# A decoder layer on one core: the down projection and final norm on token tiles of 344, 440 and 248 columns in place of three of 344

## What is computed

```
up = rmsnorm(x, g_ffn) @ w_up
upc, ffn_buf_new = causal_conv(ffn_buf, up, ffn_conv_w)
u, gt = jnp.split(upc, 2, axis=-1)
x = x + (jax.nn.silu(gt) * u) @ w_down
...
y_prompt = rmsnorm(xp, g_final)
y_sample = rmsnorm(xs, g_final)
```

## Time and profile before

| | us |
|---|---|
| median of 3 runs | 1088.61 (1086.8 to 1088.77) |
| the profiled execution, device time | 1090.33 |
| its span, first to last instruction | 1088.6 |
| TensorE busy in the span | 1063.2 (98%) |
| VectorE, ScalarE, GpSimd busy | 787.2, 511.7, 43.3 |

### The profile page before, as it was taken

One profiled execution on the slowest core, in us unless ns is written; L12 is line 12 of the kernel. 1 busy time (PEld: TensorE's weight loads), 2 busy tenths in 40 slices (PEclk: granted clock), 3 DMA queues, 4 the chain that ended last, 5 costly groups with the idle time before them and its releaser, 6 DMA issues.

```text
span 1088.6 us, 17576 instructions
## 1 busy us (share of the span) xinstructions
PE 1063.2 (98%) x6746; PEld 1031.6 (95%) x6746; DVE 787.2 (72%) x1310; ACT 511.7 (47%) x880; POOL 43.3 (4%) x165
## 2 busy tenths in 40 slices
PE   7999999999999999999999999999999999999995
PEld 6999988888999999999999999999999999999994
DVE  6954788898899888778768768777776554454457
ACT  7444344666444464454444444445444433333354
POOL 0100000000000000000000000000000000000004
PEclk9999999999999999999999999999999999999998
DMA  7311201114444112212211211311236856566504
GB/s 258 96 39 45 97 21 40 40 59 166 129 142 131 58 59 98 79 59 84 92 59 65 111 59 59 117 59 59 102 120 222 305 158 220 177 181 195 161 1 156
DMA packets 47395, 119.09 MB, mean 109 GB/s; under 512 B 5040, under 2 KB 25392, under 8 KB 47280
## 3 DMA queue, kind: packets, MB, share of 16 engines
q1 hardware_dynamic: 43904, 113.59, 31.2%
q10 hardware_dynamic: 3408, 4.38, 1.1%
HBM read 98.33 MB, written 20.66 MB: 109 GB/s over the span
## 4 chain that ended last, share of the span: by engine, by line
PE 65%; DVE 4%; issue 2%; ACT 1%; DMA 1%; SPq 1%; DVEq 0%; ACTq 0%
PE psum L2074 40%; PE psum L2098 18%; PE psum L2032 3%; PE psum L2050 2%; PE psum L1829 1%; DMA raw<-in_w 1%; DVE zb L1783 0%; PE psum L2131 0%; DVE zb L1144 0%; SPq L559 0%; SPq L625 0%; DVE x_sb L1487 0%; DVE att L1480 0%; ACT psum L1099 0%; DVE h_lo L1452 0%
## 5 line engine op out<-in xcount | busy, mean ns | idle before, releaser
L2074 PE MATMUL psum<-h_hi,w_lo 128*128 128x344 f32 x336 | 107.4, 320 | 0.0
L2074 PE MATMUL psum<-h_hi,act_lo 128*128 128x344 f32 x336 | 107.3, 319 | 0.0
L2074 PE MATMUL psum<-h_hi,act_hi 128*128 128x344 f32 x336 | 107.3, 319 | 0.0
L2074 PE MATMUL psum<-h_hi,w_hi 128*128 128x344 f32 x336 | 107.3, 319 | 0.0
L2074 PE MATMUL psum<-h_lo,act_hi 128*128 128x344 f32 x336 | 107.2, 319 | 0.0
L2074 PE MATMUL psum<-h_lo,w_hi 128*128 128x344 f32 x336 | 107.1, 319 | 0.0
L1150 DVE TENSOR_TENSOR w_lo<-raw,w_hi 128x1024 fp32r<-128x1024 f32 x50 | 61.1, 1224 | 56.1 <-ACT w_hi L726 55.8
L726 ACT ACTIVATE w_hi<-raw 128x1024 fp32r<-128x1024 f32 x51 | 53.7, 1056 | 80.0 <-PE psum L2098 58.4
L2098 PE MATMUL psum<-h_hi,w_hi 128*128 128x344 f32 x240 | 76.9, 321 | 1.2 <-DVE w_lo L1150 1.2
L2098 PE MATMUL psum<-h_hi,act_hi 128*128 128x344 f32 x240 | 77.1, 321 | 0.0
L2098 PE MATMUL psum<-h_lo,w_hi 128*128 128x344 f32 x240 | 76.7, 320 | 0.0
(11 more groups left out here) (313 smaller groups left out, 3039.0 us busy)
## 6 DMA issues: line engine op xcount, KB each, us to landing
raw<-in_w SPq DMA_DIRECT2D x111, 512.0 KB, 3.7
att<-in_w SPq DMA_DIRECT2D x26, 512.0 KB, 4.5
act_d<-att SPq DMA_DIRECT2D x20, 516.0 KB, 2.7
zb<-act_d SPq DMA_DIRECT2D x30, 344.0 KB, 4.1
x_sb<-in_x SPq DMA_DIRECT2D x8, 516.0 KB, 4.8
x_d<-x_sb ACTq DMA_DIRECT2D x12, 344.0 KB, 2.5
x_sb<-x_d SPq DMA_DIRECT2D x3, 1376.0 KB, 10.8
out_y<-x_sb SPq DMA_DIRECT2D x12, 344.0 KB, 2.5
```

Of the source, the lines that this page charges most:

```text
L2074: ins = mm(bank[to], a, b, start=(fresh and k == p == 0), stop=(k == HALF - 1 and p == 2), skip_group_check=True)
```

## The change

The down loop, the final blocks and the final norm take token tiles with edges at 0, 344, 784 and 1032: widths of 344, 440 and 248. All other parts keep tiles of 344. The number and order of instructions on each engine stay; the widths of operands and the sizes of transfers change. The running sums of squares, which lay in four places of 344 columns, lie in four of 440 (`DOWN_WIDTH`). The assertion of line 87 stays as it is and speaks of TW alone.

```
+DOWN_EDGES = (0, TW, 784, T)
+DOWN_WIDTH = max(b - a for a, b in zip(DOWN_EDGES, DOWN_EDGES[1:]))
...
-        stage = [s_flat[:, o:o + 2 * TW].rearrange("p (c t) -> p c t", c=2) for o in (0, 2 * TW)]
+        stage = [s_flat[:, o:o + 2 * DOWN_WIDTH].rearrange("p (c t) -> p c t", c=2) for o in (0, T)]
...
+        def down_tile(t):
+            return slice(DOWN_EDGES[t], DOWN_EDGES[t + 1])
+
+        def down_cols(t):
+            return slice(0, DOWN_EDGES[t + 1] - DOWN_EDGES[t])
...
-            return sq[:, g % 4, :]
+            return att[:, g % 4 * DOWN_WIDTH:g % 4 * DOWN_WIDTH + DOWN_EDGES[FIN_GROUPS[g][0] + 1] - DOWN_EDGES[FIN_GROUPS[g][0]]]
...
-                        sp.dma_start(x_sb[:, :, tile(t)], x2_d[:, :, tile(t)]).then_inc(x2_back[t], 16)
+                        sp.dma_start(x_sb[:, :, down_tile(t)], x2_d[:, :, down_tile(t)]).then_inc(x2_back[t], 16)
...
-                    ins = nc.gpsimd.tensor_tensor(x_sb[:, m, tile(t)], x_sb[:, m, tile(t)], rstd[:, tile(t)], ALU.mult)
+                    ins = nc.gpsimd.tensor_tensor(x_sb[:, m, down_tile(t)], x_sb[:, m, down_tile(t)], rstd[:, down_tile(t)], ALU.mult)
...
-                        xh, xl = h_hi[:, e + kk, tile(0)], h_lo[:, e + kk, tile(0)]
+                        xh, xl = h_hi[:, e + kk, down_cols(t)], h_lo[:, e + kk, down_cols(t)]
...
-                            ins = mm(down_ps[m], a, b, start=(g == kk == p == 0), stop=(g == DOWN_PAIRS - 1 and kk == 1 and p == 2))
+                            ins = mm(down_ps[m][:, down_cols(t)], a, b, start=(g == kk == p == 0), stop=(g == DOWN_PAIRS - 1 and kk == 1 and p == 2))
```

More of the change, by code:

```diff
@@ L458, in build @@
         job_ps = [psum[:, 512 * b:512 * b + TW] for b in range(3)]
-        fin_ps = [psum[:, 512 * b:512 * b + TW] for b in FIN_BANK]
+        fin_ps = [psum[:, 512 * b:512 * (b + 1)] for b in FIN_BANK]
+        square_ps = [psum[:, 512 * b:512 * (b + 1)] for b in range(3)]
         bank = {c: psum[:, 512 * b:512 * b + TW] for c, b in BANK.items()}
-        down_ps = [psum[:, 512 * b:512 * b + TW] for b in DOWN_BANK]
+        down_ps = [psum[:, 512 * b:512 * (b + 1)] for b in DOWN_BANK]
         gate_ps = [psum[:, 512 * b:512 * b + TW] for b in range(3, 6)]
@@ L558, in load_act @@
                     sp.wait_ge(act_split, i - 1)
-                sp.dma_start(stage[i % 2], act_d[2 * g:2 * g + 2, :, t * TW:(t + 1) * TW].rearrange("c p t -> p c t")).then_inc(act_landed[i % 2], 16)
+                sp.dma_start(stage[i % 2][:, :, down_cols(t)], act_d[2 * g:2 * g + 2, :, down_tile(t)].rearrange("c p t -> p c t")).then_inc(act_landed[i % 2], 16)
             for p in range(4):
@@ L635, in _ @@
                     sp.wait_ge(y_last_ready, n + 1 - by_pool)
-                sp.dma_start(outs["y"][:, m, tile(t)], x_sb[:, m, tile(t)]).then_inc(stored, 16)
+                sp.dma_start(outs["y"][:, m, down_tile(t)], x_sb[:, m, down_tile(t)]).then_inc(stored, 16)
             for t in range(NT):
@@ L1023, in split_act @@
                     act.wait_ge(half_done, 2 * (i - len(ENTRIES)) + 2)
-                nc.scalar.activation(h_hi[:, e:e + 2, tile(0)], stage[i % 2], ACT.Copy).then_inc(act_hi_ready, 1)
+                cols = down_cols(i // DOWN_PAIRS)
+                nc.scalar.activation(h_hi[:, e:e + 2, cols], stage[i % 2][:, :, cols], ACT.Copy).then_inc(act_hi_ready, 1)
             def split_last(c):
@@ L1093, in fin_square @@
                         act.wait_ge(fin_added, n - 2)
-                    dst = job_ps[n % 3]
+                    dst = square_ps[n % 3][:, down_cols(t)]
                 else:
@@ L1098, in fin_square @@
                     dst = fin_total(g)
-                nc.scalar.activation(dst, x_sb[:, m, tile(t)], ACT.Square).then_inc(fin_sq_ready, 1)
+                nc.scalar.activation(dst, x_sb[:, m, down_tile(t)], ACT.Square).then_inc(fin_sq_ready, 1)
             def fin_gain(t, m):
                 act.wait_ge(fin_sq_ready, KD * t + m + 1)
-                nc.scalar.activation(x_sb[:, m, tile(t)], x_sb[:, m, tile(t)], ACT.Copy,
+                nc.scalar.activation(x_sb[:, m, down_tile(t)], x_sb[:, m, down_tile(t)], ACT.Copy,
                                      scale=gain_fin[:, m:m + 1]).then_inc(fin_gain_done, 1)
@@ L1109, in fin_root @@
                 act.wait_ge(fin_sum_done, sum(u <= t for u, _ in FIN_GROUPS))
-                nc.scalar.activation(rstd[:, tile(t)], task_ps[:, 0:TW], ACT.Sqrt, bias=eps[:, 0:1],
+                nc.scalar.activation(rstd[:, down_tile(t)], task_ps[:, down_cols(t)], ACT.Sqrt, bias=eps[:, 0:1],
                                      scale=1.0 / D).then_inc(fin_root_done, 1)
@@ L1687, in act_rest @@
                 dve.wait_ge(act_hi_ready, i + 1)
-                V.tensor_tensor(h_lo[:, e:e + 2, tile(0)], stage[i % 2], f32(h_hi[:, e:e + 2, tile(0)]), ALU.subtract).then_inc(act_split, 1)
+                cols = down_cols(i // DOWN_PAIRS)
+                V.tensor_tensor(h_lo[:, e:e + 2, cols], stage[i % 2][:, :, cols], f32(h_hi[:, e:e + 2, cols]), ALU.subtract).then_inc(act_split, 1)
             def last_rest(c):
@@ L1700, in down_evac @@
                 src = down_ps[m] if n < NT * KD else fin_ps[n % 4]
-                V.tensor_tensor(x_sb[:, m, tile(t)], src, x_sb[:, m, tile(t)], ALU.add).then_inc(down_read, 1)
+                V.tensor_tensor(x_sb[:, m, down_tile(t)], src[:, down_cols(t)], x_sb[:, m, down_tile(t)], ALU.add).then_inc(down_read, 1)
             for name in FIRST_PARTS[0:3]:
@@ L1782, in fin_reciprocal @@
                 dve.wait_ge(fin_root_done, t + 1)
-                V.reciprocal(rstd[:, tile(t)], rstd[:, tile(t)]).then_inc(fin_rstd_ready, 1)
+                V.reciprocal(rstd[:, down_tile(t)], rstd[:, down_tile(t)]).then_inc(fin_rstd_ready, 1)
             def fin_add(t, m):
@@ L1793, in fin_add @@
                 total = fin_total(fin_group(t, m))
-                V.tensor_tensor(total, job_ps[n % 3], total, ALU.add).then_inc(fin_added, 1)
+                V.tensor_tensor(total, square_ps[n % 3][:, down_cols(t)], total, ALU.add).then_inc(fin_added, 1)
             def fin_scale(t, m):
                 dve.wait_ge(fin_gain_done, KD * t + m + 2)
-                V.tensor_tensor(x_sb[:, m:m + 2, tile(t)], x_sb[:, m:m + 2, tile(t)],
-                                rstd[:, tile(t)].unsqueeze(1).broadcast_to([P, 2, TW]), ALU.mult).then_inc(y_last_ready, 1)
+                V.tensor_tensor(x_sb[:, m:m + 2, down_tile(t)], x_sb[:, m:m + 2, down_tile(t)],
+                                rstd[:, down_tile(t)].unsqueeze(1).broadcast_to([P, 2, DOWN_EDGES[t + 1] - DOWN_EDGES[t]]), ALU.mult).then_inc(y_last_ready, 1)
             for t in range(NT):
@@ L2130, in fin_sum @@
                     pe.wait_ge(fin_root_done, t)
-                mm(task_ps[:, 0:TW], ones[:, :], fin_total(g), start=(ms[0] == 0), stop=(m == KD - 1)).then_inc(fin_sum_done, 1)
+                mm(task_ps[:, down_cols(t)], ones[:, :], fin_total(g), start=(ms[0] == 0), stop=(m == KD - 1)).then_inc(fin_sum_done, 1)
             for n in range(NT * KD):
@@ L2140, in _ @@
                 pe.wait_ge(down_read, KD * (NT - 1) + FIN_FREE[n] if n < 4 else NT * KD + n - 3)
-                passes(fin_ps[n % 4], [(*wslot(s, kk * 4 + m % 4), h_hi[:, 4 + kk, tile(t)], h_lo[:, 4 + kk, tile(t)])
+                passes(fin_ps[n % 4][:, down_cols(t)], [(*wslot(s, kk * 4 + m % 4), h_hi[:, 4 + kk, down_tile(t)], h_lo[:, 4 + kk, down_tile(t)])
                                         for kk in range(2)]).then_inc(down_done, 1)
```

## The result

The changed kernel takes **1091.47 us** (median of 15 runs, 1088.79 to 1093.87) where the kernel before took 1088.74 in the same comparison (15 runs, 1086.8 to 1090.03). The ratio is 1.0024, 95% interval [1.0014, 1.0034]: 2.7 us slower, in the stated range and in the direction of the forecast, whose +1.4 us is half of what was measured.

What follows compares the result with a forecast made beforehand. TensorE was taken to bound the kernel, with SyncE's store order deciding behind the last matmul. Terms 0 + 0 + 1.4 = +1.4 us move the median from 1088.61 to 1090.0 us; 8-in-10 range 1083.5 to 1094.0.

Steps and rivals of the forecast that it cites:

- The loop costs nothing: Down loop: tile 1 19.2 us longer, tile 2 19.2 us shorter, sum 0, as with any cost linear in width.
- A floor at 0.11 us: TensorE, down loop: weight loads alone pace at 0.11 us, under the 117.6 ns of a narrow matmul; term 0.
- The estimate of +2 us: Tile 2's down loop: by the skill's figures a load outlasts 248 columns, up to +3 ns on 528 narrow matmuls.
- Cover by ScalarE and DMA in the narrow tile: Tile 2's down loop: ScalarE keeps 1.4 us of waiting, DMA needs 231 GB/s; taken as 0, 5 us if cover gone.
- -6.2 us: Rival, down loop: the 14.3 ns surplus goes at 440 columns and stays at 248; 1083.8 us with the tail, chance 0.08.
- +21.1 us: Rival, TensorE in tile 2: the load sets the pace, 248 columns cost 157.6 ns too; 1111.1 us, chance 0.10.
- the rate lost below 256 columns: Rival, down loop: 248-column rounded matmuls fall to plain float32 pace, 417 ns each; +158 us, 1248 us, chance 0.10.
- The tail gains: Rival, final stores: GpSimd ends earlier than forecast, so tile 2's stores decide; -0.9 us, 1087.7 us, chance 0.12.
- Tile 1's reciprocal: VectorE, final blocks: starts 1.4 us later and takes 0.6 more, together 2.0 us.
- GpSimd's six: GpSimd, final blocks: six multiplications of tile 1 become 1.26 us longer than 5.89, so GpSimd ends 3.3 us later.
- Store 6 sets the end: SyncE, end: store 6 issues at 1082.9, everything behind it waits, 1.92 MB drain in 5.25 us; end +1.4 us.
- The last tile's own gain counts 0: Tile 2's final chain: the 0.9 us left of its gain ends before store 6's queue has drained, so counts 0.

Runs made afterwards that it cites:

- e1: Kernel before with widths 344, 440, 248 in the down loop alone, final blocks and norm at 344: 1088.88 us, ratio 1.0001.
- e6: Kernel before with the down loop alone at 344, 512 and 176 columns: 1102.91 us, ratio 1.013.
- e5: Kernel before, equal tiles, with GpSimd doing four blocks of tile 1 and VectorE four: 1088.02 us, ratio 0.9999.
- e2: Kernel before with widths 344, 440, 248 in final blocks and norm alone, down loop at 344: 1091.65 us, ratio 1.0027.
- e3: Changed kernel with two multiplications of tile 1 moved from GpSimd to VectorE: 1091.0 us, ratio 1.0021 to the kernel before.
- e4: Changed kernel with tile 2's four stores issued on ScalarE's queue: 1091.08 us, ratio 1.0021 to the kernel before.
- e10: Changed kernel with two multiplications of tile 1 moved to VectorE and tile 2's stores on ScalarE's queue: 1091.03 us, ratio 1.003 to the kernel before.
- e9: Kernel before with final blocks and norm at 248, 440, 344 columns, down loop at 344: ratio 1.0008.

## Why the prediction was right, and where it was short

- **The loop costs nothing: right.** Predicted 0, measured +0.13 us in the profile and a ratio of 1.0001 in e1. The working took the surplus of 14.3 ns as fixed and gave 197.6 and 117.6 ns; measured are 200.3 and 114.9. Between 248 and 512 columns the pace runs from 114.9 to 232.2 ns, 0.445 ns per column and about 4.5 ns on top, so the surplus is mainly a share. The step held because any cost linear in the width cancels, as it said.
- **A floor at 0.11 us: right.** The pace read from two unhindered loads is the 111.6 ns of e6. The estimate of +2 us that the prediction drew from the Trainium skill ("TensorE: Matmul & The Clock Gate", on the issue gap and the load) is not borne out: e1 shows no such loss. Its 107 ns for a load does agree with 111.6; its gap of N / 2.4 + 2.5 gives 105.8 ns at 248 columns, measured 114.9. The section states that formula for an isolated matmul, which the prediction left out, and 131 ns as measured in a stream of 512 columns; the 232.2 ns of e6 agree with neither. The load would have shown at 248 columns only if the stream had been as fast as that formula.
- **Cover by ScalarE and DMA in the narrow tile: right.** TensorE is busy for 52.00 of 52 us there, and from 990 to 1045 us no engine waited for a transfer.
- **The three rivals on the loop fell.** e1 leaves nothing of -6.2 us, of +21.1 us, or of the rate lost below 256 columns; e6 adds that a floor exists, under 114.9 ns, and that the rate is kept at 176 columns too. *The tail gains* fell too: GpSimd's plain multiplications of 440 take 1.11 us, as the slope of 2.15 ns per column said.
- **Tile 1's reciprocal: right.** Measured from the loop's end it starts 1.5 us later (1.4 predicted) and takes 2.89 in place of 2.29 (0.6 predicted).
- **GpSimd's six: this term was mis-sized.** The prediction had 1.26 us more and wrote "The stretch stays in my sum as it is". Measured: 8.21 against 5.89, +2.3. Five differences of 0.2 and the wider base of the sixth give the 1.2; the stretch beside VectorE's instruction of 880 columns grew from 0.64 to 0.89, +0.25; and two more were stretched by 0.43 each, +0.86. These two had no place in the sum, since it asked only what the narrow last tile's 0.9 us could gain at its own end and put it at 0. An earlier root sends VectorE's multiplications into the time in which GpSimd, now later and longer, is still at work. The ends follow each other as if the two took turns: VectorE's first of tile 2 ends at 1079.50, GpSimd's fifth at 1080.47, VectorE's second at 1081.00, GpSimd's sixth at 1081.97, VectorE's third at 1082.50. The sentence that named the mechanism stood beside the sum: by the Trainium skill's "SBUF — State Buffer", "Summary: rules for kernel authors", the two engines shut each other out. Rows of before and after agree (0.91 to 1.54 on GpSimd, 1.11 to 2.00, VectorE's 0.66 to 1.58), but it was applied to the one overlap of the old schedule and priced at 0.2, not to those of the new one.
- **Store 6 sets the end: right, with the size following.** Its issue moved by 4.4 us against the loop's end (from 32.5 to 36.9), not 3.3. The drain behind it took 5.53 us, not 5.25. 1.1 + 0.3 on top of 1.4 are 2.8, and the tail grew by 2.85. The last store waited for the stores ahead of it, as foretold. But the sum counted from the 1082.81 of store 8 in one execution, the one with the slowest sums: in e5 the same chain comes 1.1 us earlier. Tails of the changed final blocks (43.8 and 44.3) are 2.4 to 4.0 us longer than those of equal ones (40.3 to 41.45). That 2.85 meets the median's 2.7 so closely is in part chance.
- **The last tile's own gain counts 0: right for the end, wrong as "no effect".** The prediction took the sums at 28% under 3.71 us, 2.7; they took 1.54 in after, since the clock fell behind them. In e2 the sums took 1.1 us more than in after, and the tail was 0.5 us shorter.

What stays open: the edits to GpSimd and to the queue (e3, e4, e10) move the profile's tail by 1.0 to 1.6 us and the ratio by nothing that 6 to 11 runs tell. So it is shown that the final blocks cost the 2.7 us, and the traces show where; that GpSimd's end and the store behind it are the whole of it in the median is argued, not shown. One profiled execution of a tail with a clock that falls at different moments may not stand for the median; more executions with profiles would settle that, and were not taken. A version in which VectorE waits with tile 2 until GpSimd is done, on the changed widths, was not tried; e9 comes nearest.

## What to carry to other kernels

In this loop unequal tiles cost nothing, since the pace was linear in the width and stayed over the floor of 111.6 ns, and they gained nothing; decide by the ends alone. At an end that is a relay of engines, redraw which instructions lie beside each other once each has its new start: a shorter last stage can fall on top of an engine still busy with the stage before, and slow both. Where one queue stores in a fixed order, look at the tile ahead of the last one: everything behind its last store waits for it. And before a single profile's tail is compared with another's, look at what the clock did in it.

## What the runs showed of the hardware

- Rounded float32 matmuls of 128 x 128 at the full clock: 111.6 ns (176 columns), 114.9 (248), 157.6 (344), 200.3 (440), 232.2 (512). The bend lies between 176 and 248, at the 0.11 us that two unhindered weight loads had shown.
- Two-input multiplications on GpSimd and VectorE beside each other stretch both: 1.11 to 1.54 us (GpSimd, 440 columns) with VectorE's 0.66 to 1.58 (496 elements); 1.11 to 2.00 beside VectorE's of 880. I had expected the second engine to lose little.
- The granted clock of TensorE fell near the program's end at different moments in executions of the same final blocks: the last six sums took 1.52 us at 1.00 and 2.58 at 0.57, and 3.69 us in before at 0.55 with 344 columns. TensorE had stood idle between short bursts before it fell. In after this did not set the end; with equal tiles the tail followed the sums' end, 40.3 to 41.45 us in four profiles.
